# Feed-forward up stage on one Trainium2 core: the 21st pair by seven products, the product tiles split later

## The reference, cut to what matters

```python
D_FF = 2816

def swiglu(h, w_gu, w_down):
    gu = h @ w_gu
    g, u = jnp.split(gu, 2, axis=-1)
    return (jax.nn.silu(g) * u) @ w_down
...
    f = swiglu(rmsnorm(h, ffn1_pre_g[l]), ffn1_w_gu[l], ffn1_w_down[l])
    h = h + 0.5 * rmsnorm(f, ffn1_post_g[l])
```

## Time and profile before

| What | us |
|---|---|
| median of three executions | 1932.9 |
| lowest and highest of them | 1931.61 and 1933.02 |
| the profiled execution | 1934.5 |
| its span, first to last instruction | 1932.8 |
| PE busy in it | 1892.2 |
| DVE busy | 1232.4 |
| ACT busy | 909.8 |

### The profile page before, as it was taken

How to read it: one execution, slowest core, us unless ns; L and a number is a source line. 1 busy time by engine, 2 the same in 40 slices (tenths; PEclk the granted TensorE clock), 3 DMA queues, 4 the chain that set the end, 5 groups by cost and what they waited for, 6 DMA issues and landing times.

```text
span 1932.8 us, 27383 instructions
## 1 busy us (share of the span) xinstructions
PE 1892.2 (98%) x10976; PEld 1588.5 (82%) x10976; DVE 1232.4 (64%) x2063; ACT 909.8 (47%) x1600; POOL 90.5 (5%) x109
## 2 busy tenths in 40 slices
PE   8999999999999999999999999999999999999997
PEld 6688877888888999888878887878898788998886
DVE  5678845644467787622738989894745478787423
ACT  4355632533355333422527777983534464334321
POOL 0100000000020000000200000111200020000000
PEclk9999999999999999999999999999999999999999
DMA  7211122233323333333222221122243223233332
GB/s 280 69 52 48 56 63 69 82 98 93 99 66 109 97 100 110 90 93 90 91 83 69 66 66 55 55 77 87 66 133 108 84 80 97 89 112 99 95 90 63
DMA packets 49439, 170.65 MB, mean 88 GB/s; under 512 B 5520, under 2 KB 8080, under 8 KB 48928
## 3 DMA queue, kind: packets, MB, share of 16 engines
q1 hardware_dynamic: 48816, 166.73, 28.3%
q0 software_dynamic: 496, 2.16, 0.3%
HBM read 166.77 MB, written 2.10 MB: 87 GB/s over the span
## 4 chain that ended last, share of the span: by engine, by line
PE 87%; DVE 9%; ACT 2%; issue 1%; DMA 0%; SPq 0%; DVEq 0%; ACTq 0%
PE acc L2103 49%; PE bank L2103 13%; PE bank L2438 2%; PE bank L2439 2%; PE bank L2437 2%; PE acc L2259 2%; PE bank L2195 2%; DVE w_lo L1262 1%; PE acc L2673 1%; PE acc L2439 1%; PE acc L2438 1%; PE acc L2437 1%; PE bank L2515 1%; PE bank L2379 1%; PE bank L2486 1%
## 5 line engine op out<-in xcount | busy, mean ns | idle before, releaser
L1262 DVE TENSOR_TENSOR w_lo<-w_raw,w_hi 128x1024 fp32r<-128x1024 f32 (+2 forms) x306 | 364.9, 1198 | 254.2 <-ACT w_hi L647 249.3
L647 ACT ACTIVATE w_hi<-w_raw 128x1024 fp32r<-128x1024 f32 (+2 forms) x306 | 313.6, 1031 | 219.9 <-PE acc L2103 178.7
L2103 PE MATMUL acc<-act_hi,w_hi 128*128 128x512 f32 (+1 forms) x936 | 366.6, 392 | 17.5 <-DVE w_lo L1262 9.4
L2103 PE MATMUL acc<-act_lo,w_hi 128*128 128x512 f32 (+1 forms) x936 | 356.1, 380 | 0.0
L2103 PE MATMUL acc<-act_hi,w_lo 128*128 128x512 f32 (+1 forms) x936 | 353.4, 381 | 0.0
L2103 PEld LDWEIGHTS acc<-act_hi,w_hi 128*128 128x128 f32 x936 | 176.5, 189 | 56.2 <-issue 13.0
L2103 PEld LDWEIGHTS acc<-act_hi,w_lo 128*128 128x128 f32 x936 | 175.8, 188 | 37.2 <-issue 1.2
L2103 PEld LDWEIGHTS acc<-act_lo,w_hi 128*128 128x128 f32 x936 | 176.6, 189 | 35.8 <-issue 2.2
L2103 PE MATMUL acc<-ffn_lo,w_hi 128*128 128x512 f32 (+1 forms) x352 | 134.2, 381 | 0.0
L2103 PE MATMUL acc<-ffn_hi,w_lo 128*128 128x512 f32 (+1 forms) x352 | 134.2, 381 | 0.0
L2103 PE MATMUL acc<-ffn_hi,w_hi 128*128 128x512 f32 (+1 forms) x352 | 134.2, 381 | 0.0
(11 more groups left out here) (560 smaller groups left out, 4083.1 us busy)
## 6 DMA issues: line engine op xcount, KB each, us to landing
w_raw<-w_all SPq DMA_DIRECT2D x282, 512.0 KB, 3.6
w_raw<-w_all SPq DMA_DIRECT2D x16, 384.0 KB, 3.2
residual<-xT SPq DMA_DIRECT2D x8, 256.0 KB, 7.3
cmp_w_k<-w1k SPq DMA_DIRECT2D x1, 2048.0 KB, 8.7
cmp_w_v<-w1v SPq DMA_DIRECT2D x1, 2048.0 KB, 12.9
w_raw<-w_all SPq DMA_DIRECT2D x8, 256.0 KB, 2.6
out_t<-residual SPq DMA_DIRECT2D x16, 128.0 KB, 1.8
ret_decay<-decay POOLq DMA_DIRECT2D x4, 256.0 KB, 3.4
```

The costliest lines, as they stand in the source:

```text
L647: A(WH[:, c % HI_RING, 0:nb * P], WR[:, c % RAW_RING, 0:nb * P], ACT.Copy).then_inc(s_hi, 1)
L1262: TT(WL[:, c % RAW_RING, 0:nb * P], WR[:, c % RAW_RING, 0:nb * P], WH[:, c % HI_RING, 0:nb * P].bitcast(F32), ALU.subtract).then_inc(s_lo, 1)
L2103: ins = MM(bank[:, cols], w[:, at, k * P:(k + 1) * P], x, start=first and r == 0 and k == 0, stop=last and r == 2 and k == nb - 1)
```

## The change

Pair 20 joins the fast pairs. No tile can then be split before pair 21: tiles 0 and 1 are split ahead of the gate work of pair 21, tiles 2 and 3 behind it, and tiles 4 to 21 behind the last product, when the down projection has begun.

```diff
-FAST = [t for t in range(5, 19) if t % 3 != 1]
+FAST = [t for t in range(5, FK - 1) if t % 3 != 1]
 BEFORE_FFN = {0: 1, 3: 2}
-HIDDEN_SPLIT = {19: (range(0, 3), range(3, 5)), 20: (range(5, 9), range(9, 13)), 21: (range(13, 17), range(17, FK))}
+HIDDEN_SPLIT = (range(0, 2), range(2, 4), range(4, FK))
...
                     if t > FAST[-1]:
-                        hidden_hi(*HIDDEN_SPLIT[t][0])
+                        hidden_hi(*HIDDEN_SPLIT[0])
                     if t not in FAST:
                         split_hi(base + 2 * t + 4)
                         silu(t)
                     if t > FAST[-1]:
-                        hidden_hi(*HIDDEN_SPLIT[t][1])
+                        hidden_hi(*HIDDEN_SPLIT[1])
+                hidden_hi(*HIDDEN_SPLIT[2])
                 branch(f"ffn{n}_down", f"g_ffn{n}_post")
...
                     if t > FAST[-1]:
-                        hidden_lo(*HIDDEN_SPLIT[t][0])
+                        hidden_lo(*HIDDEN_SPLIT[0])
                     if t not in FAST:
                         gate(t)
                     if t + 2 in FAST:
                         weight_sums(t + 2)
-                    if t < FK - 1 and t > FAST[-1]:
-                        hidden_lo(*HIDDEN_SPLIT[t][1])
+                    if t > FAST[-1]:
+                        hidden_lo(*HIDDEN_SPLIT[1])
                 split_lo(base + 2 * FK + 2)
                 product(FK - 1)
-                hidden_lo(*HIDDEN_SPLIT[FK - 1][1])
+                hidden_lo(*HIDDEN_SPLIT[2])
                 branch(f"ffn{n}_down")
```

## The result

The changed kernel took **1947.4 us**, the median of 20 executions, against 1933.0 us for 20 of the kernel before: 0.7% slower by the medians and outside the forecast range. The ratio on record, 1.0037 with the interval 1.0019 to 1.0054, leaves out the changed kernel's five longest executions as slow ones; exactly these need explaining here.

| executions | us | above the lowest level |
|---|---|---|
| 7 | 1929.7 to 1932.4 | |
| 8 | 1946.4 to 1949.3 | about 17 |
| 5 | 1961.7 to 1965.3 | about 32 |

What follows compares the result with a forecast made beforehand. TensorE, busy 98% of the span, was taken as the bound. Two feed-forwards, each saving 1.25 us and losing 0.2 to a stop, give 2.1 us saved: 1930.8 us from a median of 1932.9, range 1929.8 to 1932.9.

Steps and rivals of the forecast that it cites:

- (4): Product tiles: splits move behind pair 20; PE stops about 0.2 us at the down projection's fifth tile, each feed-forward.
- rival F: From the experiments, no chance given: fast pair 20 itself, its banks or later splits bring the slower rhythm, not the stop.
- Rival D: A pause lowers PE's clock, so the down projection runs at half speed; given no chance of its own.
- (1): Pair 20 with shorter matmuls, 9.95 us for 11.20: 1.25 us saved per feed-forward, 2.5 in both, if PE doesn't wait.
- (2): Extra DVE and ACT work around pair 20 makes PE wait nowhere: priced at nothing, other end 1.24 us.
- (3): SP's queue: third down slot loaded only from pair 20's end; costs nothing, bounds 0 and 1.6 us.
- Rival A: Splits delay PE more at product tile 4; a 1.24 us stop erases the gain, 1932.9 us; chance 0.12.
- Rival B: At 0.686 us per split, DVE's backlog delays down slot 3's weights; 0.25 us slower per feed-forward, 1933.4 us; chance 0.07.
- The sum: Over both feed-forwards, the pair's 1.25 us less the stop's 0.2, twice: 2.1 us saved.

Runs made afterwards that it cites:

- one_stop: Changed kernel with the order of no_stop in its second feed-forward only, first unaltered; ratio 0.9999 on one chip, 1.0035 on another.
- no_stop: Changed kernel, low half of down slot 2's weights made behind product tile 12's low part, not ahead of the last product; 1930.5 us, again 1930.7 us.
- probe_fine: Kernel before with 24 stops in the down projections, made by memsets of 558 to 604 columns; 1934.6 us, ratio 1.0008.
- long_stop: Changed kernel with a memset of the unused sum buffer between the last product and tile 4's low part; 1932.4 us, ratio 0.9997.
- stop_before: Kernel before, pair 20 plain, with product tiles 2 to 21 split behind the last product; 1935.4 us, ratio 1.0012.
- stop_plus: Changed kernel with a short 32-column memset between the last product and tile 4's low part; 1931.5 us, ratio 0.9991.
- second_stop: Changed kernel with three chained memsets behind the last low part, so PE is also held at down slot 3; 1934.6 us, ratio 1.0003.
- late_before: Kernel before, tiles 3 to 21 split behind the last product, memset of 266 or 192 columns ahead of tile 3's low part; 1934.1 and 1934.3 us.
- changed_again: Changed kernel, unedited, run again on another chip; 1931.5 us, ratio 0.9987.
- reset: Changed kernel with four float32 one-column matmul calls behind down slot 2 in each down projection; 1933.3 us, ratio 0.9999.
- probe_reset: Kernel before with twelve rising stops in each down projection and four float32 one-column matmuls ahead of each; 1957.7 us, one execution.
- probe_free: Kernel before with 24 stops of rising length, twelve in each down projection, PE waiting for a DVE memset; 1939.4 us, ratio 1.0025.
- one_stop_b: The one_stop kernel on a fourth chip; six executions at 1929.4 to 1931.1 us, six at 1946.0 to 1950.2, ratio 1.0035.
- changed_fourth: Changed kernel, unedited, on the fourth chip, beside a repeat of no_stop; 1930.9 us, ratio 0.9987.

## Why the prediction was wrong

**The step that failed** is in (4): "PE stops here for about 0.2 us", entered into the sum by its length alone. The stop was there, at the forecast tile, released by the forecast low part, and itself cost 0.14 us. What had no term is what came after, where the prediction has "PE takes every 0.70" for a tile of three matmuls (0.80 in the turned projections): in 18 of 40 projections PE went on at 0.267 us a matmul instead of 0.233, and 130 us later that was 16 us, a hundred times the stop.

**How far its cause is settled.** By the levels of the times, counting projections:

| | projections | turned |
|---|---|---|
| changed kernel, the result | 40 | 18 |
| changed kernel, three later runs | 66 | 0 |
| *one_stop*, first projection, load held | 23 | 7 |
| *one_stop*, second projection, no load held | 23 | 0 |
| *no_stop*, no load held | 44 | 0 |
| kernel before, 182 executions beside all kernels, no load held | 364 | 0 |

The first row, the third and the last settle that this is no mere matter of the chip or the hour: beside the 25 turned projections of the result and of *one_stop*, on the same chips, the kernel before ran 58 times and never turned. That the held load is what makes the difference rests on two things. In both profiled turned projections (one execution) the rhythm begins at the third matmul behind the held one, and nowhere else. And *one_stop*, whose second projection has all of the change but the held load, shows the single level seven times and the double level never; none of the seven was profiled, so this is read from the level. In the result 5 of 13 turned executions were double; by that share, seven singles in a row have a chance of (8/13)^7 = 0.03 if both projections can turn. So **the turn comes with the held load, on good evidence, and not beyond doubt**. The 44 projections of *no_stop* bear less on it than they seem to, since no kernel beside them turned either. The second projection of *one_stop* also speaks against rival F: it has the fast pair 20, its banks and its late splits, and shows no turn.

Shown without doubt is that a held load isn't sufficient. The same code, with gaps that differ by 0.015 us at most where a profile shows them, turned in almost half of one set of projections, and in none of three others.

Still open: what decides between these. The chip doesn't (the fourth had both). The load gap is not fully excluded: in the unrounded traces the two turned loads were held to 0.491 and 0.492 us, and those with the same stop that did not turn to 0.495 to 0.506. Against a window so narrow stand the two loads of *probe_fine* at 0.491, behind other tiles and in the kernel before, which did not turn. Whether length matters, or a fast pair 20 is needed beside the held load, is open too: all kernels with other stops (*long_stop*, *stop_before*, *stop_plus*, *second_stop*, the *late_before* ones) ran where the unedited change either didn't turn or wasn't measured. Whether float32 row sums end the rhythm rests on the one turned profile.

**Rival D** was set aside because the granted clock stays at 1.00 behind a wait of 1.24 us. That observation was right; the clock is 1.00 through the slow stretch as well. The reasoning drawn from it was too wide: "the clock doesn't fall" was taken for "a pause costs only its length". And the row used to exclude it, covers 9 us around one stop in one execution, with float32 row sums 2.7 us behind it.

**Point by point, the rest.**
- (1) The pair: 9.94 us in both feed-forwards of the profiles *after* and *changed_again*, against 9.95. Right.
- (2), (3) No PE wait at pair 20 or 21, nor anywhere in 600 to 840 us. The waits behind the projection are 1.2 us for the weights' low half, as in the earlier trace rows, and two of at most 1.0: the gain hasn't moved there. Right at nothing.
- (4) S+12.45 and S+13.28 exact; the stop 0.14 us where 0.2 was said, by two terms that nearly cancel. The handover from the low part's end to the matmul was taken as 0.20 and is 0.06 (802.08 to 802.14); and the matmul behind the held one loses 0.10, which had no term.
- Rival A (1.24 us of stop): no. *long_stop* shows what half of it would have been: 0.70 us late in each projection, and 0.9 to 1.7 us above the unedited kernel's three later medians.
- Rival B: no. The 18 low parts take 10.92 us, not 12.3. In *changed_again* slot 3's low half starts at 813.26 and is needed at 815.21, with no wait. The prediction gave half of a rule for it: the Trainium skill, "VectorE: DVE Perf Modes", section "The DRAIN you can't avoid", adds at once that a next operation that is not held starts earlier. The trace agrees with that addition, 0.602 us from start to start with 0.69 from start to end.
- The sum: where nothing turns, the change gives 2.3, 3.0 and 3.0 us in the three later runs, taken from medians; 2.1 was forecast, and the intervals reach from 0.8 to 4.4 us, so the size fits and is not measured more closely than that. Without the turned executions the forecast would have held.
- The chances: 0.03 on slower, all from rival B. The likeliest outcome on the slow side had no rival at all, because each rival was built from waits that the profile lists.

**The better version** is *no_stop*: 0.9989 and 0.9984 in two groups, 3.0 and 3.2 us by the medians, highest of 22 executions 1932.51. Beside the unedited change where that did not turn it is no faster (1930.7 against 1930.9); it is better for having no upper level. It keeps both fast pairs, and its edit is order alone: weights of slot 2, needed later, go behind the tiles needed first. That it can't turn is the reading of above, not a separate proof.

## What to carry to other kernels

An operand that arrives just in time for the head of a long run of back-to-back matmuls is a risk out of proportion to its wait: the weight load is issued a whole matmul (0.23 us) ahead, so "PE hardly waits" still means a held load. The operand has to be there more than that 0.23 us ahead of its matmul (0.9 us in *no_stop*), which the order gives that puts what is needed later behind what is needed now. Judge such a change by many executions and by the levels their times form, and look at starts from one matmul to the next, since neither the list of waits nor the granted clock shows this loss. A gain of 2 us isn't worth having until the levels are gone.

## What the runs showed of the hardware

- TensorE has a second rhythm at a granted clock of 1.00: 0.2667 us for each 512-column matmul (446 steps from 802.95 to 921.88) and 0.133 for 256 columns, against 0.2333 and 0.1185, factors 1.14 and 1.13. In the two projections profiled with it, it begins at the third matmul behind one with a held weight load, lasts 130 us, and each load still follows the start of a matmul directly. At 2.4 GHz the two rhythms are 640 and 560 cycles for 512 columns. The Trainium skill, "TensorE: Matmul & The Clock Gate", section "Wait — 56ns, not 53.3ns?", gives N / 2.4 GHz and 2.5 ns from one matmul to the next at the full clock, 215.7 ns for 512 columns; the trace agrees with neither rhythm here.
- A float32 one-column matmul call is drawn as two matmuls. Four calls inside a stream of these cost 0.89 us (*reset*, *probe_reset*), the two of the row sums 0.45.
- What a held load costs at once stands in *probe_free*. Up to a load gap of 0.35 us it costs nothing. At gaps of 0.40, 0.43 and 0.46 the held matmul is on time, and the one behind it starts 0.04, 0.07 and 0.10 us late. From there on the second stays at 0.10 (0.33 instead of 0.233) and the held matmul itself comes late, by 0.02 at 0.48 and 0.07 at 0.53. It is the same whether the rhythm turns or not.
- One program on one chip showed the effect in six of twelve executions (*one_stop_b*), and 13 minutes later on that chip a kernel with the same stop in none of eleven (*changed_fourth*).
